# Three column pairs of the state-space output in seven products each, a modulation group moved, and the router product ahead of a modulation part

## What is computed

```python
    for layer in range(DEPTH):
        mod = c_act @ ada_w[layer] + ada_b[layer]
        shift1, scale1, gate1, shift2, scale2, gate2 = jnp.split(mod, 6, axis=-1)
        ...
            mix = mamba2_mixer(...)
        x = x + gate1[:, None, :] * mix
        h2 = modulate(rmsnorm(x, norm2_w[layer]), shift2, scale2)
        ffn = hier_moe(h2, ...)
        x = x + gate2[:, None, :] * ffn
```

## Time and profile before

| | us |
|---|---|
| runs, median of 3 | 3338.65 |
| runs, lowest and highest | 3330.13, 3341.79 |
| the profiled execution | 3324.59 |
| its span, first to last instruction | 3322.8 |
| state-space groups with no modulation part | 46.0 each |
| output columns, 924.8 to 1054.8 | 130.0 |
| router until the logits are turned, 1054.8 to 1075.0 | 20.2 |

### The profile page before, as it was taken

One profiled execution on the slowest core, in us unless ns is written; L12 is line 12 of the kernel. 1 busy time (PEld: TensorE's weight loads), 2 busy tenths in 40 slices (PEclk: granted clock), 3 DMA queues, 4 the chain that ended last, 5 costly groups with the idle time before them and its releaser, 6 DMA issues.

```text
span 3322.8 us, 37429 instructions
## 1 busy us (share of the span) xinstructions
PE 3179.4 (96%) x13724; PEld 2066.4 (62%) x13724; DVE 1740.0 (52%) x3517; ACT 868.8 (26%) x1777; POOL 352.1 (11%) x302
## 2 busy tenths in 40 slices
PE   7988998999999999999999999999999999999998
PEld 4743653777843555566665555555554677878887
DVE  2253225787823326987444454444468844464555
ACT  2241221333421222154222121111121622222222
POOL 1300430333200330000120000000000012000000
PEclk9999999999999999999999999999999999999999
DMA  8647787543337796111111212222222111223231
GB/s 274 212 150 240 298 313 238 155 121 83 102 124 260 293 370 170 32 38 32 51 39 51 57 51 57 57 57 57 57 68 67 32 52 51 77 70 89 83 89 64
DMA packets 427395, 397.21 MB, mean 120 GB/s; under 512 B 28080, under 2 KB 362416, under 8 KB 420048
## 3 DMA queue, kind: packets, MB, share of 16 engines
q1 hardware_dynamic: 393520, 352.60, 33.6%
q10 hardware_dynamic: 15264, 22.24, 2.1%
q0 software_dynamic: 18432, 19.98, 1.8%
HBM read 443.54 MB, written 31.92 MB: 143 GB/s over the span
## 4 chain that ended last, share of the span: by engine, by line
PE 60%; DVE 6%; DMA 3%; issue 1%; ACT 1%; SPq 0%; DVEq 0%; ACTq 0%
PE psum L754 40%; PE psum L739 5%; DVE arena L2270 3%; PE psum L1282 3%; PE psum L979 3%; DMA ring<-in_w_branch 1%; PE psum L998 1%; PE psum L1368 1%; PE psum L1398 1%; PE psum L1408 1%; PE psum L964 1%; DVE arena L2267 1%; ACT scratch L1690 1%; PE psum L846 1%; DVE scratch L2267 0%
## 5 line engine op out<-in xcount | busy, mean ns | idle before, releaser
L754 PE MATMUL psum<-arena,ring 128*128 128x384 f32 (+1 forms) x2592 | 747.5, 439 | 11.2 <-DVE arena L2267 5.1
L754 PEld LDWEIGHTS psum<-arena,ring 128*128 128x128 f32 x2592 | 492.7, 191 | 236.2 <-DVE psum L2267 11.6
L754 PE MATMUL psum<-hT,ring 128*128 128x384 f32 (+1 forms) x2176 | 621.6, 439 | 0.0
L754 PEld LDWEIGHTS psum<-hT,ring 128*128 128x128 f32 x2176 | 412.7, 190 | 183.3 <-issue 1.4
L1698 ACT ACTIVATE scratch<-psum 128x256 f32<-128x256 f32 (+1 forms) x411 | 176.1, 429 | 955.9 <-PE psum L754 809.6
L2267 DVE TENSOR_TENSOR ring<-ring 128x512 f32<-128x512 f32 (+1 forms) x336 | 222.6, 681 | 255.1 <-PE psum L754 243.5
L2267 DVE TENSOR_TENSOR psum<-psum,scratch 128x256 f32<-128x256 f32 (+1 forms) x328 | 156.0, 480 | 371.7 <-PE psum L754 271.1
L1698 ACT ACTIVATE arena<-psum 128x512 f32<-128x512 f32 (+5 forms) x430 | 200.2, 500 | 465.5 <-PE psum L739 139.3
L739 PE MATMUL psum<-hT,ring 128*128 128x512 f32 (+1 forms) x704 | 281.9, 561 | 6.0 <-DVE hT L2263 6.0
L1690 ACT ACTIVATE arena<-psum,cols 128x256 f32<-128x256 f32 (+3 forms) x280 | 131.7, 493 | 516.3 <-PE psum L979 222.8
L2270 DVE SCALAR_TENSOR_TENSOR arena<-arena,vec 128x783 f32<-128x783 f32 (+1 forms) x256 | 228.8, 894 | 9.1
(11 more groups left out here) (287 smaller groups left out, 3734.8 us busy)
## 6 DMA issues: line engine op xcount, KB each, us to landing
ring<-in_w_in SPq DMA_DIRECT2D x177, 512.0 KB, 4.1
arena<-in_moe_w SPq DMA_DIRECT2D x44, 1536.0 KB, 10.6
ring<-in_ada_w SPq DMA_DIRECT2D x96, 512.0 KB, 6.0
ring<-in_w_mod SPq DMA_DIRECT2D x48, 512.0 KB, 5.9
ring<-in_ssm_w_in SPq DMA_DIRECT2D x48, 512.0 KB, 5.4
ring<-in_w_branch SPq DMA_DIRECT2D x64, 256.0 KB, 3.2
hT<-in_moe_w SPq DMA_DIRECT2D x10, 1536.0 KB, 13.6
ring<-in_moe_w SPq DMA_DIRECT2D x10, 1024.0 KB, 6.2
```

The costliest lines, as they stand in the source:

```text
L754: mm = nc.tensor.matmul(flat(bank_, nb), lhs[:, k, :], rhs(k), start=(start and k == 0), stop=(k == kd_ - 1), skip_group_check=True)
```

## The change

1. Output columns 0 and 1 stay as they were, but the parts between which `ssm_y(7, 1)` and the norm stand are cut otherwise. Columns 2 to 7 become three pairs n = 1, 2, 3, each of seven products (`out_product`, 8 matmuls of 128x256): `out_first(n)` and `out_rest(n)`. A pair takes four ring tiles and frees all four behind its last product.
2. GpSimd makes the weight sums of a pair (`out_sums_of`, four adds of 128x1024), VectorE the sums of the activations once (T1 to T4), into hT and free places of the arena. T1 stands ahead of `y_normed(7)`.
3. Quad 5 leaves the output columns and is put beside the state-space pairs (3, 0), (3, 2), (4, 0) and (4, 2); it is turned in iteration g = 4 of the loop. Bank 7 is kept for g < 5, before g < 2.
4. In the router of layer 1 `quad_part(8, 1)` stands behind the router product and `token_rows(0)`, no more ahead of them.
5. SP's order follows: quad 5's loads go into the input's, experts 0 to 3 stay ahead of columns 4 and 6.

The core of the diff:

```diff
-        QUAD_PAIR = {(1, 0): (7, 0), (1, 1): (7, 1), (1, 2): (7, 2), (2, 0): (7, 3)}
+        QUAD_PAIR = {(1, 0): (7, 0), (1, 1): (7, 1), (1, 2): (7, 2), (2, 0): (7, 3),
+                     (3, 0): (5, 0), (3, 2): (5, 1), (4, 0): (5, 2), (4, 2): (5, 3)}
+        QUAD_DONE = {1: 7, 4: 5}
...
             def moe(l):
-                quad_part(QUAD_MOE[l], 1)
+                if not l:
+                    quad_part(QUAD_MOE[l], 1)
...
                 token_rows(0)
+                if l:
+                    quad_part(QUAD_MOE[l], 1)
                 quad_part(QUAD_MOE[l], 2)
                 quad_part(QUAD_MOE[l], 3)
...
+            def out_product(bank_, lhs, rhs, start, name):
+
+                for k in range(8):
+                    mm = nc.tensor.matmul(bank_[:, 0:S // 2], lhs[:, k, :], rhs(k), start=(start and k == 0), stop=(k == 7),
+                                          skip_group_check=True)
+                mm.then_inc(tensor_done, pe.step(name))
+
+            y_half = lambda k0, h: lambda k: yT[:, k0 + k, S // 2 * h:S // 2 * h + S // 2]
+
+            def out_first(n):
+
+                ws = [take(("w", n, i)) for i in range(4)]
+                x = job("outM", 2 * n + 1, "x")
+                out_product(x[0], ws[0][0], y_half(0, 0), True, ("Q1", "M", n))
+                two["M", n] = ws, x
+
+            def out_rest(n):
+
+                ws, x = two["M", n]
+                w = job("outM", 2 * n, "x")
+                eng.wait_ge(vector_done, pe.at(("yn", 15)))
+                out_product(w[0], ws[1][0], y_half(8, 0), True, ("Q2", "M", n))
+                eng.wait_ge(scalar_done, pe.at(("copy_1", "ssm", "M", n)))
+                eng.wait_ge(gpsimd_done, pe.at(("S2", "M", n)))
+                eng.wait_ge(vector_done, pe.at(("T2", "M")))
+                out_product(x[0], out_sums[:, 8:16, :], lambda k: y_sum[1][:, k // 2, k % 2, :], False, ("Q6", "M", n))
+                z = job("ssm_z", "M", n)
+                eng.wait_ge(gpsimd_done, pe.at(("S1", "M", n)))
+                eng.wait_ge(vector_done, pe.at(("T1", "M")))
+                out_product(z[0], out_sums[:, 0:8, :], lambda k: y_sum[0][:, k // 2, k % 2, :], True, ("Q5", "M", n))
+                eng.wait_ge(scalar_done, pe.at(("copy_2", "ssm", "M", n)))
+                eng.wait_ge(gpsimd_done, pe.at(("S3", "M", n)))
+                eng.wait_ge(vector_done, pe.at(("T3", "M")))
+                out_product(x[0], ws[2][0], y_half(0, 1), False, ("Q7", "M", n))
+                eng.wait_ge(scalar_done, pe.at(("copy_3", "ssm", "M", n)))
+                eng.wait_ge(gpsimd_done, pe.at(("S4", "M", n)))
+                out_product(z[0], ws[1][0], y_half(8, 1), False, ("Q3", "M", n))
+                eng.wait_ge(vector_done, pe.at(("C22", "ssm", "M", n)))
+                eng.wait_ge(vector_done, pe.at(("T4", "M")))
+                out_product(x[0], ws[3][0], lambda k: y_sum_4[k // 4][:, k % 4, :], False, [x[1]] + [w_[1] for w_ in ws])
...
-                    st["kept"] = g < 2
+                    st["kept"] = g < 5
...
-                    if g == 1:
-                        quad_turn(7)
+                    if g in QUAD_DONE:
...
-                out_part(1, 0, 14)
+                out_part(1, 0, 3)
                 ssm_y(7, 1)
-                out_part(2, 0, 7)
+                out_part(1, 3, 9)
                 norm_sum(("g", 7), src_n=2)
-                out_part(2, 7, 14)
-                for c in range(3):
+                out_part(1, 9, 14)
+                out_first(1)
+                for c in range(2):
                     out_part(c, 14, 16)
-                for c in range(3, 8):
-                    if c == 4:
-                        b, full = job("ss", ("b2", 0), "c")
-                        for k in range(KD):
-                            eng.wait_ge(scalar_done, pe.at(("sq_ctx", k)))
-                            mm = nc.tensor.matmul(b[:, 0:L], ones[:, :], hT[:, k, S:S + L], start=(k == 0), stop=(k == KD - 1))
-                        mm.then_inc(tensor_done, pe.step(full))
-                    if c >= 4:
-                        quad_part(5, c - 4)
-                    out_part(c, 0, 16)
-                quad_turn(5)
+                out_rest(1)
+                b, full = job("ss", ("b2", 0), "c")
+                for k in range(KD):
+                    eng.wait_ge(scalar_done, pe.at(("sq_ctx", k)))
+                    mm = nc.tensor.matmul(b[:, 0:L], ones[:, :], hT[:, k, S:S + L], start=(k == 0), stop=(k == KD - 1))
+                mm.then_inc(tensor_done, pe.step(full))
+                for n in (2, 3):
+                    out_first(n)
+                    out_rest(n)
...
                         expert_put(1, c - 4, c - 3)
-                    if c >= 4:
-                        quad_put(5, c - 4)
                     if c == 7:
...
+                for i in (1, 2, 3):
+                    part_copy("M", 1, i)
...
-                squares("n2_1", lambda k: xT[:, k, :], lambda k: (quad_out(5) if k == 7 else None, eng.wait_ge(vector_done, ac.at(("xM", k)))))
+                out_squares = lambda first, n: squares("n2_1", lambda k: xT[:, k, :], lambda k: eng.wait_ge(vector_done, ac.at(("xM", k))), n=n, first=first)
+                part_copy("M", 2, 1)
+                out_squares(0, 4)
+                part_copy("M", 2, 2)
+                part_copy("M", 2, 3)
+                part_copy("M", 3, 1)
+                out_squares(4, 2)
+                part_copy("M", 3, 2)
+                part_copy("M", 3, 3)
+                out_squares(6, 2)
...
+                        y_side = lambda k0, h: yT[:, k0:k0 + 8, S // 2 * h:S // 2 * h + S // 2].rearrange("p (a b) n -> p a b n", b=2)
+                        eng.wait_ge(vector_done, ve.own())
+                        tt(y_sum[0], y_side(0, 1), y_side(0, 0), ALU.subtract).then_inc(vector_done, ve.step(("T1", "M")))
                         y_normed(g)
-                for c in range(8):
+                        eng.wait_ge(vector_done, ve.own())
+                        tt(y_sum[1], y_side(8, 1), y_sum[0], ALU.subtract).then_inc(vector_done, ve.step(("T2", "M")))
+                        eng.wait_ge(vector_done, ve.own())
+                        for q in range(2):
+                            tt(y_sum_4[q].rearrange("p (a b) n -> p a b n", b=2), y_side(8, 0)[:, 2 * q:2 * q + 2], y_sum[1][:, 2 * q:2 * q + 2],
+                               ALU.subtract).then_inc(vector_done, ve.step(("T4", "M")))
...
+                out_add(0)
+                eng.wait_ge(tensor_done, ve.at(("full",) + jobname("outM", 1, "x")))
+                tt(yT[:, 0:8, S // 2:S], yT[:, 8:16, S // 2:S], yT[:, 0:8, S // 2:S], ALU.subtract).then_inc(vector_done, ve.step(("T3", "M")))
+                out_add(1)
+                for n in (1, 2, 3):
...
+                    c22("M", n)
+                    c12("M", n)
+                    out_add(2 * n)
+                    eng.wait_ge(vector_done, ve.at(("C22", "ssm", "M", n)))
+                    out_add(2 * n + 1)
...
+                if n > 1:
+                    used("Q5", n - 1)
+                g_.tensor_tensor(out_sums[:, 0:8, :], b0, b1, ALU.add).then_inc(gpsimd_done, po.step(("S1", "M", n)))
+                eng.wait_ge(gpsimd_done, po.own())
+                if n > 1:
+                    used("Q6", n - 1)
+                g_.tensor_tensor(out_sums[:, 8:16, :], out_sums[:, 0:8, :], a0, ALU.subtract).then_inc(gpsimd_done, po.step(("S2", "M", n)))
+                g_.tensor_tensor(b0, a0, b0, ALU.subtract).then_inc(gpsimd_done, po.step(("S3", "M", n)))
+                used("Q2", n)
+                eng.wait_ge(gpsimd_done, po.at(("S2", "M", n)))
+                g_.tensor_tensor(a1, a1, out_sums[:, 8:16, :], ALU.subtract).then_inc(gpsimd_done, po.step(("S4", "M", n)))
+
             for i in range(1, 8):
```

More of the change, by code:

```diff
@@ L374, in program @@
         rb = mE.take(1)
+        out_sums_from = mE.at
         rt = mE.take(4, 36)
@@ L381, in program @@
         held_at = MODW - 5 * EW
-        assert mE.at <= held_at
+        assert mE.at <= held_at and out_sums_from <= held_at - 2060 and at_e >= 16 * S and at_e + D <= routed_at
         in_thirds = lambda t: [t[:, 0:D], t[:, D:2 * D], t[:, 2 * D:3 * D]]
@@ L425, in program @@
         SSM_PAIRS = (("B", "C"), ("x0", "x1"), ("z0", "z1"))
+        y_sum = [hT[:, 0:4, 0:S].rearrange("p a (b n) -> p a b n", b=2), hT[:, 4:8, 0:S].rearrange("p a (b n) -> p a b n", b=2)]
+        y_sum_4 = [arena[:, o:o + 4 * (S // 2)].rearrange("p (k n) -> p k n", k=4) for o in (at_e, routed_at + ROUTE_W)]
+        out_sums = arena[:, held_at - 2060:held_at - 2060 + 2 * D].rearrange("p (k n) -> p k n", n=P)
         def pair_jobs(g, n):
-            if g == "A":
-                return jobname("inA", 2 * n, "x"), jobname("inA", 2 * n + 1, "x")
+            if g in ("A", "M"):
+                return tuple(jobname("in" + g if g == "A" else "out" + g, c, "x") for c in (2 * n, 2 * n + 1))
```

(19 more changed lines are left out.)

10 lines of the change are left out of this document (6 added, 4 removed).

## The result

The changed kernel takes 3340.61 us (median of 12 runs, 3333.76 to 3345.61). In the same session the kernel before took 3330.45 us (median of 12, 3325.74 to 3341.79); the ratio on record is 1.0025, 95% interval 1.0014 to 1.0036. The two medians lie 10.2 us apart, and the ratio says some 8 us. That is less than the 0.3% that were counted as no change, but the interval does not reach 1.0000: the kernel is slower. That the 3337.3 us of the forecast lay near the measured time is luck: it was set from the median of the three runs shown, 8 us above what the kernel before gives over twelve. What was forecast was the difference, -1.3 us, and that failed.

The account below looks back on a forecast made before the run. TensorE bounds the output columns and state-space iterations; VectorE paces the router product and the chain behind the logits. Up to `norm_sum` -10.5 us, router +9.2: -1.3 from 3338.65 gives 3337.3 us, range 3327 to 3347.

Parts of the forecast that it names:

- Four are taken out here and put beside the state-space pairs: Output columns: moving quad 5's four parts, 2.06 us each, to the equally full state-space stage changes nothing, 0 us.
- a wait for loads in iterations g = 2 and 3: State-space stage: a TensorE wait for loads there was listed as showing the forecast wrong; no size given.
- 9.05: Router: logits 9.2 us later against the router product, less 0.15 us won by quad 5's turn leaving.
- The four tiles: Router: part 3's four loads reuse part 1's slots and take 7.0 us from freed to landed, between 5.5 and 10.2.
- air: Router product: 1.1 us of slack against VectorE's pace, so beginning at half clock costs only 0.3 us.
- Part 3 at half clock: Router: after its wait, quad 8's part 3 takes 3.47 us, that is 1.79 + 1.68.
- not late: Router: part 3 lands behind part 2 after all, only part 1's 1.79 us is added; -8.7 us, chance 0.15.
- seven products bring nothing: Output pairs: banks or waits eat the saving of the eighth product; +8.7 us, 3347, chance 0.06.
- GpSimd holds the pairs: Output pairs: products wait for GpSimd's weight adds; mild case +11 us, three times slower adds about 47 slower; chance 0.07.
- The router gives back more than the columns gain: Router: four loads needing over about 8.3 us make the kernel slower, +2.7 at the upper bound; chance 0.14 beyond 1 us.
- 0.13 for "slower": Whole kernel: chance of being slower by more than about 0.3% (10 us); faster had 0.15, same 0.72.
- -9.95, -1.26 and +0.9: Seven-product output pairs save 9.95 us, the vanished wait ahead of column 7 1.26; quad 5's turn in state-space costs 0.9.

Follow-up runs that it names:

- a second placing of quad 5: The changed kernel with quad 5's parts beside pairs (3,0), (3,1), (3,2) and (4,0), turned in g = 3: 1.0024 of the kernel before.
- the best kernel: The changed kernel with quad 5's last part at (5,0), quad 8's part 1 ahead of the router product, output tiles freed one by one: 3319.92 us, 0.9973.

## Why the prediction was wrong

**The wait that was not foreseen: 7.7 us.** The step that failed reads "Four are taken out here and put beside the state-space pairs, where TensorE is just as full: 0." The parts do cost nothing more there (50.29 and 48.20 us with two and one). But a part also takes four of the eight ring slots, and I named no cover for that. Beside (4,2) it made the tiles of (5,1) so late that GpSimd's adds of them began 11 us later. GpSimd has time in plenty, and so I looked for no wait there. But the adds now lie over VectorE's steps at the start of the iteration, and each of these then lasts about as long as an add: the four TENSOR_SCALAR steps 1.35 to 1.49 us instead of 0.28 to 0.48. Behind them on VectorE stand its additions in PSUM (line 2327), for which TensorE's next product waits. Shorter adds (47.04 us) and another place for the part (49.49 us with a part in it) each take the wait away. The prediction named "a wait for loads in iterations g = 2 and 3" as a sign of being wrong; the loads were late one iteration further on, and for GpSimd.

The Trainium skill, page "SBUF — State Buffer", section "Who interferes with whom", names `tensor_scalar` among the operations that can enter VectorE's modes with both port pairs, and says that the engine which comes second is then held for a whole instruction, not slowed. The two traces agree: 0.28 us of work became 1.35, the length of an add. I cited that section for operations with two SBUF inputs only, and only for the output pairs. There the same thing does happen and has cover: T1 lasts 4.32 us beside an add, where T2, of the same size, takes 2.29 with no add beside it; TensorE is busy throughout:

```profile
970.38 4.32 DVE L2327 TENSOR_TENSOR hT<-arena 128x2048 f32<-128x2048 f32 x1
```

The kernel before had a trace of it too, which I did not read: at 797.90 a TENSOR_SCALAR of 128x384 took 0.77 us beside an add, and 0.41 where it had none beside it.

**The router was seen, and priced too low: 11.5 us for 9.05.** Of the 9.05 us, 0.2 were for slower logits and lie behind the mark that is measured here, so 2.6 us are to be explained. Three terms of that sum:
- The four tiles: 8.2 us from the end of part 1 to part 3's start, not 7.0: 1.2 us. The windows of 1 us in the changed kernel show why:

```profile
1079.00:1080.00 1.00, 0.61 (x8) 0.00 (x0) 0.00 (x0) 0.00 (x0) 0.00 (x0) 1.00 0.78 117
1080.00:1081.00 1.00, 0.00 (x0) 0.00 (x0) 0.00 (x0) 0.00 (x0) 0.00 (x0) 1.00 0.97 367
...
1084.00:1085.00 1.00, 0.00 (x0) 0.00 (x0) 0.00 (x0) 0.00 (x0) 0.00 (x0) 0.67 0.97 356
```

  Part 1 ends near 1077.8, the bytes run from about 1079.3 to 1085.0, nearly as in my working, and then 1.0 us more pass before part 3 starts at 1086.04. I had left out the time from the last byte to TensorE's start.
- The product: 9.69 us instead of 8.09. TensorE is idle for 3.6 us ahead of it, and the granted clock is 0.50 from 1065 to 1069. It ended 3.0 us after VectorE's last hT, where it was 1.5 before: 1.5 us, for which I had 0.3. My "air" of 1.1 us was reckoned at the full clock. The size of this term is not fixed: behind the same 3.60 us the product took 8.80 us in the kernel with the router edit alone, and 8.72 with quad 5's last three parts earlier; what decides between 8.7 and 9.7 stays open.
- Part 3 at half clock: 3.57 us by the starts, forecast 3.47. The granted clock from 1086 to 1088 is 0.50, the level of 1.2 GHz. The prediction cited the Trainium skill, page "TensorE: Matmul & The Clock Gate", section "Part 1: The HAM clock gate (the "warmup" mystery)", for an array at half rate until its own activity has released the clock, and this trace agrees.

The idle TensorE ahead of the last part, forecast at "about 5 us", was 6.42; from the product's end to the logits 14.7 us, forecast 12 to 15. Behind the logits 0.6 us came back, where I had written that nothing would: from them to TensorE's first work on the gathered rows (line 964 before) it is 25.57 us, before 26.17.

**The rest held.** Pairs of 24.2 us without a wait, a stage of 110.5 us, 10.0 us for the seven products, quad 5 otherwise neutral (1.0001). The rivals "not late" and "seven products bring nothing" are refuted. "GpSimd holds the pairs" named the right engine at the wrong place and with the wrong victim: what it held was VectorE, and through it TensorE. "The router gives back more than the columns gain" came about, 11.5 us against some 10, though the four tiles took 8.2 us, just under the 8.3 of that rival: the product added the rest. That alone would be a change of about 1 us; it is the 7.7 us that make the kernel slower beyond its interval. (The 0.13 for "slower" were the last two rivals' chances by themselves, so this one's tail stood at nothing in them.)

**The account.** From the start of g = 0 to the columns' end the changed kernel took 463.64 us, before 465.44: -1.8, where -10.3 was forecast (-9.95, -1.26 and +0.9); the difference is the 7.7 us of g = 4 and 0.8 spread over the rest. With +11.5 and -0.6 it is +9.1 us in these two executions. With the 5.1 ahead of g = 0 that leaves 1.0 of the 15.2 us of the spans, behind the router, which is not accounted for. The ratio says 8.3, with 4.7 to 12.0 by its interval.

## What to carry to other kernels

When work with loads is moved from one full stage to another, price three things: its instructions, the slots that its tiles take from the loads behind it, and what the engine that uses those later tiles will then run beside. An engine with time to spare can still cost: when its work shifts by some us it may fall beside steps of another engine that it holds up, and here 11 us of shift on GpSimd made 7.7 us on TensorE. And where an operand's slot is the next load's slot, order the code by when slots come free. Three edits, one part of quad 5 one pair later, a part of quad 8 run before the wait and not behind it, and tiles given back after their last product, turned a loss of 8 us into a gain of 9.

## What the runs showed of the hardware

- GpSimd and VectorE hold each other instruction by instruction: TENSOR_SCALAR of 128x128 to 128x512 in float32 takes 0.28 to 0.48 us alone, 1.35 to 1.49 us beside adds. GpSimd's adds of 128x512 take 1.27 us alone and up to 1.60 beside those steps, and 2.54 us where one starts beside a VectorE TENSOR_TENSOR of 128x1280 (1.49 us). With adds of 128x32 the same VectorE steps took as long as alone.
- An idle TensorE paid twice in these traces. Behind a wait of 4.49 us one product of eight passes took 3.78 us instead of 1.89, behind 6.42 us a part took 3.64 instead of 1.92, behind 3.30 us (a second placing of quad 5) 3.45, and behind 2.88 us 3.12. Behind 1.52 us (the best kernel's router product, 8.17 us at a granted clock of 1.00) nothing was lost.
- Four tiles of 512 KB, issued when their slots came free, needed 8.2 us until the first product that reads them, of which 5.7 were transfer.

Not tried: the logits ahead of parts 2 and 3 of quad 8, which would want the parts' copy moved on ScalarE as well; and the pairs without any move of quad 5, which are known here only as the difference of two kernels.
